# Odd attention: one reciprocal per pair of heads, and one masked addition over 256 columns

## The reference, cut to what matters

```
def forgetting_attention(q, k, v, log_f):            # heads 0 to 7
    fcum = jnp.cumsum(log_f, axis=-1)
    ...
        logits = einsum('bhqd,bhkd->bhqk', q_i, k) * ATTN_SCALE
        logits = logits + f_i[..., :, None] - fcum[..., None, :]
        logits = where(kpos[None, :] <= qpos[:, None], logits, -inf)
        p = softmax(logits, axis=-1)
        return einsum('bhqk,bhkd->bhqd', p, v)
def moba_attention(q, k, v, rel_bias):               # heads 8 to 15
    # 256 tokens are one block: causal attention with a T5 bias by distance
    logits = q @ k * ATTN_SCALE + bias, masked; p = softmax(logits); p @ v
```

## Time and profile before

| | |
|---|---|
| median of 3 runs | 1242.11 us (1241.94 to 1242.13) |
| the profiled execution | 1241.86 us |
| its span, first to last instruction | 1240.2 us |
| PE busy | 1226.8 us, 99% |
| DVE busy | 967.9 us, 78% |
| ACT busy | 703.7 us, 57% |
| POOL busy | 135.2 us, 11% |
| granted TensorE clock | 1.000 over the span |

### The profile page before, as it was taken

The page is one execution under the profiler, slowest core; times in us unless marked ns, Lnnn a source line. Parts: engine busy times, 40 slices in busy tenths (PEclk is TensorE's granted clock), DMA queues, the critical chain, the costliest instruction groups (busy, mean ns, idle before and its releaser), DMA issues.

```text
span 1240.2 us, 18559 instructions
## 1 busy us (share of the span) xinstructions
PE 1226.8 (99%) x7013; PEld 1062.9 (86%) x7013; DVE 967.9 (78%) x1218; ACT 703.7 (57%) x1061; POOL 135.2 (11%) x249
## 2 busy tenths in 40 slices
PE   8999999999999999999999999999999999999998
PEld 7989888888778989998889888888888998888887
DVE  5868999977885798898788688997685898676654
ACT  6555555556465555555677566555564243755552
POOL 5000000010000211111132201120010010000000
PEclk9999999999999999999999999999999999999999
DMA  9746777665562798893132348997466597386540
GB/s 325 236 153 218 241 248 238 223 200 180 186 202 68 235 329 311 313 334 115 55 120 71 137 169 293 392 392 261 170 200 208 171 316 259 124 291 212 179 161 34
DMA packets 153649, 265.77 MB, mean 214 GB/s; under 512 B 6092, under 2 KB 110480, under 8 KB 153584
## 3 DMA queue, kind: packets, MB, share of 16 engines
q1 hardware_dynamic: 134560, 204.75, 48.9%
q0 software_dynamic: 18544, 59.65, 13.6%
q10 hardware_dynamic: 480, 0.49, 0.1%
HBM read 263.78 MB, written 1.08 MB: 214 GB/s over the span
## 4 chain that ended last, share of the span: by engine, by line
PE 87%; DVE 8%; ACT 2%; issue 2%; POOL 1%; DMA 0%; POOLq 0%; ACTq 0%; DVEq 0%
PE ps L1949 24%; PE ps L1929 17%; PE ps L1932 9%; PE ps L1915 4%; PE ps L1914 4%; PE ps L1913 4%; DVE w_lo L1142 2%; PE ps L1992 2%; PE ps L1994 2%; PE ps L1993 2%; PE ps L2056 2%; PE ps L1970 2%; PE ps L1972 2%; PE ps L2058 2%; PE ps L1971 2%
## 5 line engine op out<-in xcount | busy, mean ns | idle before, releaser
L1142 DVE TENSOR_TENSOR w_lo<-raw,w_hi 128x2048 fp32r<-128x2048 f32 (+3 forms) x211 | 434.1, 2072 | 32.2 <-ACT w_hi L580 31.9
L580 ACT ACTIVATE w_hi<-raw 128x2048 fp32r<-128x2048 f32 (+3 forms) x213 | 368.7, 1737 | 61.7 <-PE ps L1949 51.1
L1929 PE MATMUL ps<-xn,w_hi 128*128 128x512 f32 x976 | 244.7, 393 | 0.1
L1929 PEld LDWEIGHTS ps<-xn,w_hi 128*128 128x128 f32 x976 | 178.2, 188 | 35.5 <-issue 1.6
L1932 PEld LDWEIGHTS ps<-xn,w_lo 128*128 128x128 f32 x976 | 133.1, 190 | 9.6
L1932 PE MATMUL ps<-xn,w_lo 128*128 128x256 f32 x976 | 136.1, 282 | 0.0
L1949 PE MATMUL ps<-w_hi,a_hi 128*128 128x512 f32 x432 | 134.6, 393 | 0.2 <-DVE a_lo L1854 0.2
L661 ACT ACTIVATE work<-ps 128x512 f32<-128x512 f32 x61 | 36.3, 595 | 171.7 <-PE ps L1932 171.7
L1949 PE MATMUL ps<-w_lo,a_hi 128*128 128x512 f32 x432 | 133.5, 390 | 0.0
L1949 PE MATMUL ps<-w_hi,a_lo 128*128 128x512 f32 x432 | 133.2, 389 | 0.0
L1913 PE MATMUL ps<-xn,w_hi 128*128 128x256 f32 x432 | 122.6, 284 | 0.0
(11 more groups left out here) (362 smaller groups left out, 2006.6 us busy)
## 6 DMA issues: line engine op xcount, KB each, us to landing
raw<-in_ffn_w SPq DMA_DIRECT2D x64, 1024.0 KB, 5.5
side<-in_ada_w POOLq DMA_DIRECT2D x96, 512.0 KB, 6.1
raw<-in_ffn_w_in SPq DMA_DIRECT2D x40, 1024.0 KB, 5.2
raw<-in_ffn_w_out SPq DMA_DIRECT2D x32, 512.0 KB, 5.2
raw<-in_gm_w_in SPq DMA_DIRECT2D x16, 1024.0 KB, 6.4
raw<-in_od_w_in SPq DMA_DIRECT2D x12, 1024.0 KB, 5.5
raw<-in_gm_w_out SPq DMA_DIRECT2D x8, 1024.0 KB, 5.5
raw<-in_ev_w_in SPq DMA_DIRECT2D x7, 1024.0 KB, 13.3
```

The costliest lines, as they stand in the source:

```text
L580: nc.scalar.activation(w_hi[s][:, 0:w], raw[s][:, 0:w], ACT.Copy).then_inc(hi_done, 1)
L1142: nc.vector.tensor_tensor(w_lo[s][:, 0:w], raw[s][:, 0:w], w_hi[s][:, 0:w].bitcast(F32), ALU.subtract)\
L1929: nc.tensor.matmul(o, hi, xn[:, 512 * k:512 * k + 512], start=k == 0, stop=False)
```

## The change

The reciprocals of a pair's four row sums (two heads by two query tiles) are taken in one instruction, which now waits for both heads' exponentials; the four multiplications follow. For heads 0 to 7 the second query tile's 256 columns get decay and mask in one instruction instead of two, with a mask tile `at_mask` of 256 columns, zeros and then the causal mask, that POOL makes once. The numbers in the waits on `s_sb` follow, and `half_ready` is now `made`, with DVE waiting once for 3.

```
+        at_mask = acc[:, 4, 768:1024]
...
             def at_probs(i):
-                dve.wait_ge(AT["exp"], 2 * i + 2)
+                dve.wait_ge(AT["exp"], 2 * i + 4)
                 c, one_over = 34 + 4 * (i % 4), 48 + 2 * (i % 4)
-                chain(nc.vector.reciprocal(st[:, one_over:one_over + 2], st[:, c:c + 2]))
-                for t, (c0, c1) in enumerate(SEG):
-                    s = at_sb[i % 4][:, c0:c1]
-                    nc.vector.tensor_scalar(s, s, st[:, one_over + t:one_over + t + 1], None, ALU.mult).then_inc(AT["p"], 1)
+                sums = st[:, c:c + 8].rearrange("p (h t) -> p h t", h=2)[:, :, 0:2]
+                chain(nc.vector.reciprocal(st[:, one_over:one_over + 4].rearrange("p (h t) -> p h t", h=2), sums))
+                for n in (i, i + 1):
+                    for t, (c0, c1) in enumerate(SEG):
+                        s, k = at_sb[n % 4][:, c0:c1], 48 + 2 * (n % 4) + t
+                        nc.vector.tensor_scalar(s, s, st[:, k:k + 1], None, ALU.mult).then_inc(AT["p"], 1)
...
                 s, bank = at_sb[i % 4], at_bank(i)
+                if i == 0:
+                    dve.wait_ge(made, 3)
                 if i < FOX:
                     f = [zf[:, 4, 8 * t + i:8 * t + i + 1] for t in range(TT)]
                     nc.vector.scalar_tensor_tensor(s[:, 0:P], bank[:, 0:P], f[0], causal, ALU.add, ALU.add).then_inc(AT["s_sb"], 1)
-                    nc.vector.tensor_scalar(s[:, P:2 * P], bank[:, P:2 * P], f[1], None, ALU.add).then_inc(AT["s_sb"], 1)
-                    nc.vector.scalar_tensor_tensor(s[:, 2 * P:3 * P], bank[:, 2 * P:3 * P], f[1], causal, ALU.add, ALU.add)\
+                    nc.vector.scalar_tensor_tensor(s[:, P:3 * P], bank[:, P:3 * P], f[1], at_mask, ALU.add, ALU.add)\
                         .then_inc(AT["s_sb"], 1)
-                    dve.wait_ge(AT["s_sb"], 3 * i + 3)
+                    dve.wait_ge(AT["s_sb"], 2 * i + 2)
...
-            for i in range(4):
+            for i in (0, 2):
                 at_probs(i)
...
                 if 2 <= i < HEADS - 2:
                     at_probs(i + 2)
-                    at_probs(i + 3)
...
             pool.wait_ge(rows_out, 16)
+            nc.gpsimd.memset(at_mask[:, 0:P], 0.0).then_inc(made, 1)
+            pool.wait_ge(in_cst, 16)
+            nc.gpsimd.tensor_copy(at_mask[:, P:], causal).then_inc(made, 1)
             pool.dma_start(flip, I["consts"][:, C_ALL:].bitcast(F32R)).then_inc(bias_in, 16)
```

More of the change, by code:

```diff
@@ L359, in build @@
         vec_ps, vec_ready, cs_ready = sem("vec_ps"), sem("vec_ready"), sem("cs_ready")
-        rb_ready, half_ready, rows_ps, rows_sb, rows_out = sem("rb_ready"), sem("half_ready"), sem("rows_ps"), sem("rows_sb"), sem("rows_out")
+        rb_ready, made, rows_ps, rows_sb, rows_out = sem("rb_ready"), sem("made"), sem("rows_ps"), sem("rows_sb"), sem("rows_out")
         bias_in, ctx_in = sem("bias_in"), sem("ctx_in")
@@ L2240, in at_scores @@
                     if 4 <= n < FOX + 4:
-                        pe.wait_ge(AT["s_sb"], 3 * (n - 4) + 3)
+                        pe.wait_ge(AT["s_sb"], 2 * (n - 4) + 2)
                     elif n >= 4:
@@ L2302, in _ @@
                     pe.wait_ge(fold_done, 1)
-                    pe.wait_ge(AT["s_sb"], 12)
+                    pe.wait_ge(AT["s_sb"], 8)
                     fold_out(od_red, 3, 384).then_inc(ada_ps, 1)
@@ L2666, in _ @@
                 pool.dma_start(stage[p:p + m, r, :], src).then_inc(in_later, 16)
-            nc.gpsimd.memset(half[:, :], -0.5).then_inc(half_ready, 1)
-            pool.wait_ge(half_ready, 1)
+            nc.gpsimd.memset(half[:, :], -0.5).then_inc(made, 1)
+            pool.wait_ge(made, 1)
             row_rstd("ev")
```

## The result

The changed kernel takes 1244.30 us (median of 20 runs), the kernel before 1241.88 us (20 runs beside them). The ratio is 1.0018, with a 95% interval from 1.0012 to 1.0025: slower by 2.4 us. That it is slower is beyond doubt; the size, 0.18%, is only known to lie between 0.12 and 0.25%. The profiled execution of the changed kernel has a span of 1242.5 us, against 1240.2. Two of all the executions behind this page stood far out, one of the kernel before at 4328.01 us and one of e2 at 1732.38 us with a granted clock of 0.656; no reading rests on them.

The account below looks back on a forecast made before the run. The prediction took PE to bound the kernel, with a closed PE, ACT and DVE loop in the attention; 2.33 us of later weights less 0.26 for the mask gave +2.07, so 1244.2 us, range 1242.4 to 1245.4.

Parts of the forecast that it names:

- The loop: Attention rounds from head 8 on: PE, ACT and DVE steps sum to the 3.52 us round; a delay returns every round.
- The reciprocal for a pair: Attention on DVE: second head's weights come 0.46 to 0.47 us later in five pairs, (4,5) to (12,13); 2.33 us in all.
- The pairs without cost: Pairs (0,1) and (2,3), covered by DVE's wait for PE, and (14,15), with 0.55 us of slack: nothing added.
- The mask: One 256-column addition for two of 128 on DVE: 0.13 us gained a head, only heads 6 and 7 counting, 0.26 us.
- The reciprocal's own cost: DVE's reciprocal of four values in place of two: taken as the same 0.17 us; at worst +0.85 us over five pairs.
- The dear reciprocal: Rival: four values cost twice two, another 0.17 us every round on the loop; +2.9 us, 1245.0 us; chance 0.07.
- POOL: POOL's memset and copy near 275.25 us, beside DVE's scaling before PE's transposes: taken as 0, at worst +0.3 us.
- The sum: Whole kernel: 2.33 − 0.26 = +2.07 us, giving 1244.2 us, 0.17% slower; the forecast's chance 0.72.
- the shift at 347 us: Sign at the attention's start: the forecast would be wrong if the shift there were already other than zero.
- DVE's pace: Rival: DVE bounds the attention, so fewer masks and reciprocals make it faster by 0.9 us, 1241.2 us; chance 0.05.
- the delay that doesn't add up: Rival: attention rounds absorb the late weights, only the first two pairs and one round count; +1.1 us, 1243.2; chance 0.13.
- The falling clock: Rival: PE's idle time drops its clock to 1.2 GHz for three rounds; of the order of +10 us, 1252; chance 0.03.

Follow-up runs that it names:

- e2: Changed kernel with a reciprocal for each head as before, so the 256-column mask alone; 1241.82 us against 1242.01 for the kernel before.
- e6: Kernel before with the reciprocal for a pair in pair (8,9) alone; 1242.35 us in one run, against 1242.09 for the kernel before.
- e1: Kernel before with the reciprocal for a pair alone, old masks and no work on POOL; 1244.35 us against 1242.01.
- e3: Kernel before with only the wait of the first head's reciprocal moved to the second head's exponentials; 1245.30 us against 1242.01.
- e7: Kernel before with the reciprocal for a pair in pair (14,15) alone; 1241.95 us in one run, against 1242.09 for the kernel before.
- e10: Kernel before with only the first head's reciprocal wait moved to the second head's exponentials, measured a second time; 1245.71 us against 1241.90.

## Why the prediction was right

- **The loop.** Putting 0.47 into it gave 3.99. e6 shows it for a single pair, e1 for all. The argument for it in the prediction is weaker than it reads: steps from one start to the next, from the exponentials of one pair to those of the next, add up to the round whatever they are. What carried it is that each step starts as the one before ends, with only 0.03 us before the reciprocal and 0.06 before PE; and the step from PE to ACT's copy has a second thing in it, the copy of the pair's first head, which ends as the transposes do.
- **The reciprocal for a pair.** 2.33 predicted, 2.35 measured in e1's profile and 2.34 in its time. That the wait, not the instruction, is the cost was argued in the prediction and shown by e3.
- **The pairs without cost.** (14,15) shown by e7. (0,1) and (2,3) were not tried alone, but e1's profile shows no cost: PE has no wait for DVE before their transposes, which start 0.43 us ahead of the copy of the values and 2.79 us behind it, in place of 0.43 and 2.80.
- **The mask.** 0.26 predicted, 0.25 measured in e2. The instruction takes 0.476 us, the value read from its like the earlier trace rows; the estimate of 392 ns by the Trainium skill, "VectorE: DVE Perf Modes", section on the TRN2 errata, does not agree with it. That only heads 6 and 7 count shows in e2's profile: head 5's transposes start 6.83 us after the copy of the values, as before, and head 7's 11.23 us after it in place of 11.48.
- **The reciprocal's own cost.** 176 ns for four values, 163 for two: the step from its start to the multiplications went from 0.20 to 0.21. The dear reciprocal is out.
- **POOL.** Taken as 0, measured as 0.1; it lay inside the bound of 0.3. The way was another: not the scaling beside POOL's copy, which no PE work felt, but a later cast beside a load's issue that POOL's work had pushed back.
- **The sum.** +2.07 for the stretch, 2.08 measured. The medians differ by 2.42, of which 2.18 are the stretch and POOL. The last 0.24 is within the interval of the comparison (1.5 to 3.1 us) and as large as the spread of the kernel before's own medians (1241.88 to 1242.11); it is not settled. That the time came out at 1244.30 where 1244.2 was forecast is in part luck: the difference was 0.35 larger than forecast, and the kernel before ran 0.23 faster than in its first three runs.
- **The upper bound.** It was summed wrongly. Mask, reciprocal and POOL all at their worst are 2.33 + 0.18 + 0.85 + 0.3 = +3.7, not +3.4; that would have been 1245.8 us, above the stated range. Nothing came near it.
- **Signs that failed.** The prediction called itself wrong if the shift at 347 us were other than zero. It was 0.30, and the shift behind the attention 2.38 in place of 2.1. The sign was badly chosen: that copy moves by 0.9 us between profiles of kernels that are the same there or nearly so, and only differences within one profile can be read to 0.1 us. The wait of 0.4 to 0.7 us before a pair's transposes holds in the rounds alone; in pairs (4,5) and (6,7) it is 1.41 and 1.53, because PE waited there before as well (0.52 and 0.95 us ahead of the first head of these pairs).
- **The rivals.** DVE's pace, the delay that doesn't add up and the dear reciprocal are excluded by e1, e3 and e6. The falling clock was not the case in the changed kernel's profile, but it is in both profiles of the kernel with the later wait (e3, e10), which has only 0.20 us more idle time in each pair; its chance of 0.03 rested on too little, the one stretch at 85%. Its price, of the order of 10 us, was too high as well: one fall made the stretch 0.7 to 0.8 us longer.

## What to carry to other kernels

Merging two small instructions saves their fixed cost once, but the merged one waits for the later input: on an engine that waits anyway, ask how much of the work behind it used to run inside that wait. Look for a loop across engines in which each step starts when the one before it ends; what is put into it counts in every round, and what runs beside it is free as long as it stays shorter than the wait that it fills. That a chain of steps adds up to the round proves nothing, since any chain does; look at the gaps, and then delay one round on purpose, as e6 does. Splitting work so that each piece waits for less, here twice the reciprocals, made the stretch 0.9 us shorter, but it helps only until the engine's own queue becomes the limit, and that must be worked out for the tightest pair and not for the usual one.

## What the runs showed of the hardware

- PE's granted clock fell to 0.5 for 3.4 us in both profiles of the kernel with the later wait, from 361.5 us in e3's and from 361.0 in e10's, after 8 us (353 to 361) in which PE was busy for 5.11 us; the fall made the stretch 0.7 to 0.8 us longer. The Trainium skill, "TensorE: Matmul & The Clock Gate", Part 1, says that the clock follows PE's recent activity and has two levels; the rows agree with both.
- A POOL copy of 128 columns took 0.57 us beside DVE's scaling, which took 0.92 in place of 0.88, and 2.13 us beside a DVE split, which was not longer for it.
- A DVE cast of 256 columns took 0.44 to 0.46 us in place of 0.29 in the five profiles in which POOL issued a bias load beside it; beside most other issues of POOL the same cast took its usual time.
